# A two-block transformer forward pass: the dense layer's three matrix products as seven products of quarters

## The reference

```python
def swiglu(h, w_gate, w_up, w_down):
    return (jax.nn.silu(h @ w_gate) * (h @ w_up)) @ w_down
...
        x = x + g1 * mix
        h = rms_norm(x, g_norm_ffn[l]) * (1 + sc2) + sh2
        if l % 2 == 0:
            y = swiglu(h, ffn_w_gate[l // 2], ffn_w_up[l // 2], ffn_w_down[l // 2])
...
        x = x + g2 * y
```

## Time and profile before

| | |
|---|---|
| median of 3 runs | 2409.84 us (2399.26 to 2415.98) |
| profiled execution: its own time | 2407.22 us |
| its span, first to last instruction | 2405.1 us |
| TensorE busy in the span | 2310.4 us, 96% |
| VectorE, ScalarE, GpSimd busy | 836.4, 386.5, 27.8 us |
| mean granted TensorE clock | 0.979 of full speed |
| the dense layer | 243.4 to 480.7 us of the span |

### The profile page before, as it was taken

How to read it: one execution, slowest core, us unless ns; L and a number is a source line. 1 busy time by engine, 2 the same in 40 slices (tenths; PEclk the granted TensorE clock), 3 DMA queues, 4 the chain that set the end, 5 groups by cost and what they waited for, 6 DMA issues and landing times.

```text
span 2405.1 us, 35152 instructions
## 1 busy us (share of the span) xinstructions
PE 2310.4 (96%) x15101; PEld 1612.7 (67%) x15102; DVE 836.4 (35%) x2039; ACT 386.5 (16%) x903; POOL 27.8 (1%) x52
## 2 busy tenths in 40 slices
PE   7989999999999999999999899899899999989999
PEld 4768888877764444444443444377589998659999
DVE  3663634138420000000000000134566742557663
ACT  3222100022320000000000000023521002442101
POOL 1010000000100000000000000000000000000000
PEclk9998999999899999999999999999999999999999
DMA  9473587632169999889999999973124463323441
GB/s 362 148 266 117 193 316 278 223 106 99 44 248 383 370 409 412 311 331 409 411 408 412 408 410 411 399 249 115 43 91 161 170 210 107 122 71 101 162 160 52
DMA packets 225519, 582.92 MB, mean 242 GB/s; under 512 B 19899, under 2 KB 79811, under 8 KB 213077
## 3 DMA queue, kind: packets, MB, share of 16 engines
q1 hardware_dynamic: 224788, 580.52, 64.4%
q0 software_dynamic: 576, 0.13, 0.0%
HBM read 579.58 MB, written 1.05 MB: 241 GB/s over the span
## 4 chain that ended last, share of the span: by engine, by line
PE 86%; DMA 5%; DVE 4%; SPq 2%; ACT 2%; issue 1%; DVEq 0%; ACTq 0%
PE wrk L2347 12%; PE acc L862 9%; PE wrk L1592 6%; PE acc L2407 5%; PE acc L3126 5%; PE acc L3158 5%; PE wrk L2332 4%; PE acc L865 4%; PE wrk L3158 4%; PE wrk L3126 4%; DMA ring<-in_moe_w_down_dram 3%; PE acc L1609 3%; PE wrk L2354 3%; PE acc L936 2%; PE acc L2390 2%; PE acc L951 2%
## 5 line engine op out<-in xcount | busy, mean ns | idle before, releaser
L2347 PE MATMUL wrk<-ring,hT 128*64 128x512 f32 (+1 forms) x1792 | 348.4, 542 | 8.1 <-DMA ring<-in_moe_w_up_dram 4.8
L2591 DVE TENSOR_TENSOR scratch<-scratch,wrk 128x512 f32<-128x512 f32 (+4 forms) x32 | 24.6, 767 | 804.7 <-PE wrk L2347 598.5
L2347 PEld LDWEIGHTS wrk<-ring,hT 128*64 128x64 f32 x1792 | 126.3, 137 | 205.6 <-issue 187.0
L862 PE MATMUL acc<-hT,ring 128*128 128x256 f32 (+2 forms) x1152 | 262.7, 385 | 1.3 <-ACT scratch L892 0.5
L862 PEld LDWEIGHTS acc<-hT,ring 128*128 128x128 f32 (+2 forms) x1152 | 210.7, 186 | 42.6 <-issue 4.4
L2407 PE MATMUL acc<-ring,scratch 128*64 128x512 f32 x784 | 177.7, 597 | 15.2 <-DMA ring<-in_moe_w_down_dram 15.2
L3203 DVE TENSOR_TENSOR ring<-ring 128x512 f32<-128x512 f32 (+1 forms) x192 | 155.3, 864 | 1.2
L1592 PE MATMUL wrk<-hT,ring 128*128 128x256 f32 x704 | 154.8, 380 | 0.0
L1592 PEld LDWEIGHTS wrk<-hT,ring 128*128 128x128 f32 x704 | 132.8, 190 | 18.6 <-ACT hT L748 0.9
L2407 PEld LDWEIGHTS acc<-ring,scratch 128*64 128x64 f32 x784 | 54.0, 136 | 117.1 <-issue 102.5
L3158 PE MATMUL acc<-scratch,ring 128*128 128x128 f32 x1024 | 117.6, 275 | 0.0
(11 more groups left out here) (438 smaller groups left out, 2714.3 us busy)
## 6 DMA issues: line engine op xcount, KB each, us to landing
ring<-in_moe_w_gate_dram SPq DMA_DIRECT2D x56, 2048.0 KB, 22.0
ring<-in_moe_w_up_dram SPq DMA_DIRECT2D x56, 2048.0 KB, 20.8
ring<-in_moe_w_down_dram SPq DMA_DIRECT2D x56, 2048.0 KB, 20.4
ring<-in_w_ada_dram SPq DMA_DIRECT2D x24, 2048.0 KB, 14.8
ring<-in_w_up_dram SPq DMA_DIRECT2D x32, 1024.0 KB, 7.4
ring<-in_w_down_dram SPq DMA_DIRECT2D x32, 1024.0 KB, 6.6
ring<-in_w_out_dram SPq DMA_DIRECT2D x8, 2048.0 KB, 8.0
ring<-in_w_in_dram SPq DMA_DIRECT2D x8, 1536.0 KB, 12.7
```

Source lines behind the costliest of these rows:

```text
L862: mm = pe.matmul(acc[p0:p0 + m, bank, 0:S], cols(k), hT[:, k, :], start=(k == 0), stop=(k == KD - 1))
L2347: mm = pe.matmul(flat_wrk[h * HD:h * HD + HD, lo:lo + n2], hT[:, k, 0:HD], w[:, at_, h * n2:(h + 1) * n2], start=(k == 0), stop=(k == KD - ...
```

## The change

The three matrix products of the dense layer are done by Winograd's form of Strassen's scheme. Each matrix is cut into quarters: the width in two halves, the 2816 columns in two halves of 1408, the tokens in two halves of 128. In place of eight products of quarters there are seven, numbered 1 to 7. Four of them have a sum of weights as the stationary operand (t1 to t4, each the difference of two quarters or of a quarter and another sum), and four a sum of activations as the moving one.

The work is cut into eighteen steps (`dense_step`): twelve rises, gate and up in turn for each of six units, and six falls for the down weights. A unit is two tiles of 128 columns in each half, the last unit one tile; so steps 0 to 9 and 12 to 16 are full and steps 10, 11 and 17 are half as large. A full step has 7 x 2 x 4 = 56 products of 128 x 128 with 128 tokens. All eighteen steps together have 924 products, 1848 rows in a trace.

Each step takes two places of the ring: the item with its weights, loaded by two transfers, and a `room` without a load, into which the four sums of weights are written. Of these sums GpSimd makes t1 and t3 (`dense_pool`), which need the loaded weights only, and VectorE makes t2, which needs t1, and t4, which needs t2 (`d_weight_sums_dve`). The fourteen blocks of w_ada stay with VectorE, one behind each of the steps in `DENSE_ADA_AT`; four of their sums stay late.

```diff
+DENSE_ADA_AT = (0, 1, 3, 4, 6, 7, 9, 10, 11, 12, 13, 14, 15, 16)
...
+            for n in range(3 * D_UNITS):
+                kind, u = dense_step(n)
+                out += [(kind, u), (kind + "room", u)]
+                out += [("ada", *DENSE_ADA[i]) for i, step in enumerate(DENSE_ADA_AT) if step == n - 1]
...
+        def dense_pe(pe):
+            for n in range(D_RISES + D_FALLS):
+                for i in d_adas(n - 2):
+                    if i not in LATE_SUMS:
+                        ada_pe(pe, *DENSE_ADA[i])
+                if n == D_RISES + D_FALLS - 1:
+                    for i in d_adas(n - 1):
+                        ada_pe(pe, *DENSE_ADA[i])
...
+        def dense_pool(pool):
+
+            for n in range(D_RISES + D_FALLS):
+                raw = d_blocks(n)
+                pool.wait_ge(*landing(d_item(n)))
+                pool.wait_ge(*free_of(PLACE[d_room(n)] - SLOTS))
+                for out_, a, b in ((d_weight_sum(n, 1), raw[0, 1], raw[0, 0]), (d_weight_sum(n, 3), raw[1, 1], raw[0, 1])):
+                    if n < D_RISES:
+                        pool.tensor_tensor(out_, a, b, ALU.subtract).then_inc(d_first_sums, 1)
+                    else:
+                        for t in range(d_pairs(d_unit(n))):
+                            ins = pool.tensor_tensor(out_[:, t], a[:, t], b[:, t], ALU.subtract)
+                        ins.then_inc(d_first_sums, 1)
...
+            for out_, a, b, wait in ((t2, raw[1, 1], t1, (d_first_sums, 2 * n + 1)), (t4, raw[1, 0], t2, (d_weight_sums, 2 * n + 1))):
+                dve.wait_ge(*wait)
+                for t in parts:
+                    ins = dve.tensor_tensor(out_[:, t], a[:, t], b[:, t], ALU.subtract)
+                ins.then_inc(d_weight_sums, 1)
...
+        def d_combine_dve(dve, n):
...
+            dve.tensor_tensor(z_(0, 0), p2, first, ALU.add).then_inc(d_combined, 1)
+            if n + 1 < D_RISES + D_FALLS:
+                d_weight_sums_dve(dve, n + 1)
+            dve.wait_ge(d_produced, 6 * n + 4)
+            dve.tensor_tensor(v2, p6, first, ALU.add).then_inc(d_combined, 1)
...
+            dve.wait_ge(freed_by_pe, freeing(d_room(n)))
+            dve.tensor_tensor(z_(0, 1), p4, v3, ALU.add).then_inc(d_combined, 1)
...
         def dense_dve(dve):
...
+            d_token_sums_dve(dve)
+            d_weight_sums_dve(dve, 0)
+            for n in range(D_RISES + D_FALLS):
+                if n < D_RISES:
+                    d_combine_dve(dve, n)
+                    if n == D_RISES - 1:
+                        d_act_sums_dve(dve, 0)
+                elif n + 1 < D_RISES + D_FALLS:
+                    d_weight_sums_dve(dve, n + 1)
+                    d_act_sums_dve(dve, n + 1 - D_RISES)
+                for i in d_adas(n):
+                    ada_dve(dve, *DENSE_ADA[i])
+            ada_end_dve(dve, 1, 8, 11)
             ada_end_dve(dve, 1, 0, 3)
             ada_end_dve(dve, 0, 10, 11)
+            dense_end_dve(dve)
```

More of the change, by code:

```diff
@@ new lines, in dense_fall_pe @@
+        def dense_fall_pe(pe, f):
+            n = D_RISES + f
+            stationary, sums = d_stationary(n), d_act_sums(f)
+            low, high = (d_acts(f)[:, h] for h in range(2))
+            moving = {1: low[:, :, 0:P], 2: high[:, :, 0:P], 3: sums[:, 3], 4: high[:, :, P:S], 5: sums[:, 0], 6: sums[:, 1], 7: sums[:, 2]}
+            last = f == D_FALLS - 1
+            pe.wait_ge(*landing(d_item(n)))
+            pe.wait_ge(ffn_act, d_tiles(f))
+            for x in LAST_ORDER if last else UP_ORDER:
+                d_weights_pe(pe, n, x)
+                if x in (3, 5, 6):
+                    pe.wait_ge(d_act_sums_done, 4 * f + {5: 1, 6: 3, 3: 4}[x])
+                if f == 0:
+                    pe.wait_ge(d_combined, 7 * (D_RISES - 1) + LAST_READ[x])
+                for t in range(d_pairs(f)):
+                    for m in range(4):
+                        mm = pe.matmul(PRODUCT[x][:, m * P:(m + 1) * P], stationary[x][:, t, m, :], moving[x][:, t, :],
+                                       start=(f == 0 and t == 0 and m == 0), stop=(last and t == d_pairs(f) - 1), skip_group_check=True)
+                if last and x != LAST_ORDER[-1]:
+                    mm.then_inc(d_fallen, 1)
+            mm.then_inc(freed_by_pe, 2)
@@ new lines, in d_tiles, with d_adas @@
+        def d_tiles(u):
+            return 2 * sum(d_pairs(i) for i in range(u + 1))
+        def d_adas(n):
+            return [i for i, step in enumerate(DENSE_ADA_AT) if step == n]
+        def dense_pe(pe):
+            for n in range(D_RISES + D_FALLS):
[6 more added lines that the diff above has]
+                if n < D_RISES:
+                    dense_rise_pe(pe, n)
+                else:
+                    dense_fall_pe(pe, n - D_RISES)
@@ new lines, in d_weight_sums_dve @@
+        def d_weight_sums_dve(dve, n):
+            raw = d_blocks(n)
+            t1, t2, t4 = (d_weight_sum(n, i) for i in (1, 2, 4))
+            parts = [slice(None)] if n < D_RISES else list(range(d_pairs(d_unit(n))))
+            for out_, a, b, wait in ((t2, raw[1, 1], t1, (d_first_sums, 2 * n + 1)), (t4, raw[1, 0], t2, (d_weight_sums, 2 * n + 1))):
[3 more added lines that the diff above has]
+                ins.then_inc(d_weight_sums, 1)
```

295 lines of the change are left out of this document (193 added, 102 removed).

## The result

| | before | changed |
|---|---|---|
| median of the runs | 2410.76 us (4 runs) | 2444.24 us (2439.22 to 2447.6, 4 runs) |
| ratio, 95% interval | | 1.0144 (1.0121 to 1.0166) |
| profiled execution: span | 2405.1 us | 2442.1 us |
| the dense layer | 237.3 us | 249.0 us |
| mean granted clock | 0.979 | 0.964 |

The change makes the kernel 33 us slower where I forecast 8. The direction was right, the size is outside the range of 2391 to 2437.

A forecast was written before the change was run, and what follows sets the result against it. TensorE was taken to bound the kernel, busy throughout the dense layer. Terms -21.6 + 5 + 17 + 1.7 + 3.6 + 2 gave +7.7 us on 2407.2, so 2415 and a median of about 2417; 80% range 2391 to 2437.

The forecast's parts named there:

- The products: Dense layer: 1848 rows of TensorE at 0.1116 us, 206.3 us, replace 1056 rows of 227.9 us; -21.6 us.
- The mechanism: VectorE instructions with two SBUF inputs and GpSimd's sums of weights wait for each other's end; VectorE rows reading PSUM are free.
- The rises and the start: Steps 0 to 9: VectorE late at paired w_ada blocks, +5 us; layer start: GpSimd meeting the norm, later sums, +1.7 us.
- From step 10 to the last fall: VectorE and GpSimd one after the other need 101.6 us against TensorE's 78.2; +17 us, bounds +4 and +25.
- The clock: TensorE's rows slow down after gaps, mainly the one in front of the last fall; +2 us (0 to 8).
- The end: Behind the last product VectorE still has additions and residual rows, so the next norm starts later; +3.6 us (1 to 5).
- The forecast's layer: Dense layer forecast at 235 to 246 us, against 237.3 before and a floor of 215.7.
- Rival 1: VectorE slips in between GpSimd's long instructions in the dense layer: stage 219.4 us, kernel 2393, median 2396; chance 20%.
- Rival 2: TensorE's mean clock falls under 0.85 in steps 12 to 17: 24 us on top, 2441 us; chance 12%.
- Rival 3: The ring: w_ada blocks land late in the dense layer and VectorE waits for them; +14 us, 2431 us; chance 8%.

The follow-up runs named there:

- e1: Changed kernel with VectorE making all four sums of weights, GpSimd none; 2414.44 us, 1.0014 of the kernel before.
- e3: Changed kernel with GpSimd's sums cut to a single column each, all waits and VectorE's work kept; 2407.44 us, part left out, dense layer 226.4 us.
- e6: Changed kernel with seven products in the rises alone, falls in eight, VectorE making all sums of weights; 2406.87 us, 0.9981 of the kernel before.
- e7: Kernel with seven products in the rises alone, w_ada blocks at every other rise step and more in the falls; 2404.52 us, 0.9975 of before.
- e9: Kernel with seven products in the rises alone and w_ada spread out, now no block at steps 9 and 10; 2400.77 us, 0.9962 of before.
- e8: Changed kernel with throwaway TensorE products in its longest waits, half as many as in a first try; 2433.99 us, 1.0109 of the kernel before.
- e10: Seven products in the rises alone, no w_ada block at steps 9 and 10, seven blocks in the rises, seven in the falls; 2400.67 us, 0.9964 of before.
- e5: Changed kernel with throwaway TensorE products in front of its longest waits, which proved longer than the gaps; 2438.17 us, 1.0111 of the kernel before.

## Why the prediction was wrong

**The products, -21.6: right.** Steps 1, 4 and 7 of the changed kernel, which have no gap and no slow rows, take 12.50 to 12.51 us each, the forecast's 12.50.

**The mechanism, right; its reach, too narrow.** I counted VectorE's instructions with two SBUF inputs and looked for them in the dense layer alone. The rows of the attention have one input in SBUF, and they waited too: 2.27 us for 128x2, 4.63 for two of 128x128. The Trainium skill had the piece that I left out ("SBUF — State Buffer", section "Who interferes with whom"): `tensor_scalar` can run in a mode that takes both of VectorE's ports and then contends with GpSimd as well. The trace agrees that such rows wait; which mode they ran in it doesn't show. I wrote that steps 0 to 2 "are summed before the layer" and charged step 2 alone: **6.4 us left out**, put at nothing: the first step that failed. (The longest wait in my own rows was also 0.55 us and not 0.43: the 48-column row issued at 596.27 waited until 596.82.)

**The rises and the start: +5 and +1.7; 12.8 measured**, 1.6 in the norm and 140.96 - 129.8 = 11.2 in the steps, of which 5.2 are gaps and 6.0 slow rows. The gaps are as forecast, though not for the reason of paired blocks only: GpSimd's sums come in clumps of two steps on one block, because the items land in clumps.

**From step 10 to the last fall: +17; 21.2 measured**, 99.4 - 78.2, of which 13.1 are gaps and 8.1 slow rows. Where they lie I had wrong. I had put 14.7 us a step on every fall; steps 14 to 16 run at 13.3 to 13.5, since each sum of GpSimd costs 0.9 us and not 1.17. The gaps are at steps 11 to 13, the turn, where two blocks of w_ada, a combining chain of half-wide steps that covers nothing and the first falls' sums follow each other: 1.8, 4.5 and 3.4 us. The first is not GpSimd's, as it is 1.8 us in e1, e3 and e6 too. The second is 1.9 in e3, without GpSimd's work, and the third isn't there. In the kernels with falls of eight products, moving the blocks (from e7 to e9) takes the gaps at the turn away.

**The clock: +2 (0 to 8).** This is the term of the sum that was most mis-sized, the second step that failed: 16.5 us of slow rows in the layer, its last fall among them, which takes 8.7 us instead of 6.2, and 2.9 us in the norm behind it. What they cost is less: 4.4 us in the layer and 2.6 in the norm by e8, 7.0 together, and up to 5.6 more that e8 left slow. I had charged one gap; there are six of 1.8 to 4.5 us in the layer and one of 4.4 ahead of the norm.

**The end: +3.6; 4.5 measured.** Right, but behind the 4.4 us of idle TensorE the norm's products take 6.28 us instead of 3.62, with a granted clock of 0.71 between 503.3 and 518.0 us, and the norm's 2.9 us belong to this step.

**The forecast's layer** was 215.7 + 5 + 17 + 2, some 240 us; it is 249.0. Taking it apart by e8: 214.2 of products, 24.8 of waiting for VectorE, filled or not, where I had 22 and 1.5 for the start, and 10.0 of slow rows that were on the path or may have been, where I had 2. So the waiting was sized about right in sum, and the clock is what the layer's forecast had wrong.

Attention 6.4, start 1.6, layer 11.7, end 4.5 and norm 2.9 make 27.1 us of the 33.5 between the medians. **The cause of the other 6.4 stays open.** They lie in stretches without a changed instruction, ahead of the picks and in the second block. From the norm behind the layer to the end, the eleven other traces take 1928.2 to 1934.5 us and that of before 1924.5. The granted clock goes with it: in that stretch it is at the lower of its two levels for 61 us in the trace of before and for 69 to 88 us in the eleven others. Of the 61 runs of before, those at a mean granted clock of 0.979 take 2405.3 us on average and those at 0.976, the median, 2410.7, so the profile of before, at 0.979, was a lucky one. The medians of e6, e7 and e10 are 2 to 3 us above what their layers alone would make them, and their median clocks are 0.974, 0.975 and 0.974. Why these runs were granted less in unchanged stretches, none of mine says.

Rival 1 is out: rows of w_ada last up to 2.73 us, stage 249. Rival 2 said the right thing of the wrong steps: the clock is 0.92 from step 10 on and not under 0.85, and steps 14 to 16 run fast. Rival 3's sign came true in part: GpSimd waited 125 us in the layer for landings, VectorE for none. It is out as a price of its own, as TensorE's list of waits names VectorE for every long gap; what remains of it is that landings set when GpSimd's sums meet VectorE's.

## What to carry to other kernels

In these traces, work given to GpSimd is taken off VectorE only where VectorE idles or reads PSUM; beside VectorE's SBUF work it costs most of its length, and GpSimd is slower at it (2.34 us against 1.19 for the same sum). So ask of every sum on GpSimd which rows of VectorE it will meet, also those of the stage before, where it runs as soon as its data is there; one wait moved it into a pause and gave about 7 us by the traces, 11 by the medians. And of a scheme that trades TensorE's work for VectorE's, take the half in which VectorE has time: seven products in the rises, with VectorE's blocks placed for them, are worth 10 us here, in the falls they cost more than they save (2414.4 with them, 2406.9 without).

## What the runs showed of the hardware

- Turn-taking is by whole instruction, and both sides lose. The line of GpSimd's sums in the falls (shortest, median and longest ns) shows it from the other side; in the timeline, two of the same size beside rows of VectorE that read PSUM take 1.25 us each:

```profile
L1731 POOL TENSOR_TENSOR ring<-ring x22: 1294/1710/1801, 408.9 to 478.4; 128x512 f32<-128x512 f32 x22
```

```profile
393.21 2.50 POOL L1728 TENSOR_TENSOR ring<-ring 128x512 f32<-128x512 f32 x2 [13.69 <-DMA ring<-in_ffn_w_up_dram]
```

- A meeting costs less than the full length: 7.9 us for four instructions of 2.34, 3.55 us for four of 1.25. So some 0.36 us of each cost nothing; why, no run shows. The Trainium skill ("SBUF — State Buffer", section "Who interferes with whom") says the loser blocks for the whole instruction; the rows agree but for that part.
- A `tensor_scalar` with one input in SBUF waits too, however small: 128x2 took 2.27 us in the attention, and a w_ada block's first row (L706) 1.22 us instead of 0.48 at 356.10 us, beside GpSimd.
- Rows of VectorE with an input in PSUM don't wait (0.42 us for 128x256 in the attention, beside GpSimd), nor does the reciprocal of 128x256 (1.75 us with and without GpSimd).
- TensorE's clock stayed at 2.4 GHz through gaps of 0.6 and 0.8 us in e7 (granted 1.00). After the gaps of 2.2 to 4.5 us of the changed kernel, that of 1.9 ahead of its last fall and that of 1.0 in e9, the rows ran for some microseconds at or near the lower level, 1.2 GHz, as in the 5.34 us above; after one of 1.8 us in the changed kernel and one of 2.1 in e7 they didn't. So the length of the last gap alone doesn't tell. With throwaway rows in the gaps the layer's mean granted clock was 0.99 (e5, e8) against 0.95.
